# Two transformer blocks in fp32 on one Trainium2 core: layer ends taken token group by token group

## The chip, the cores and the metric

The kernel runs on one core of one Trainium2 chip. Its metric is the device time of one execution in microseconds (us), the median of several runs. Before the change it is 2314.95 us, over three runs from 2311.51 to 2321.45.

A core has these engines: TensorE (PE in the profile) for matrix products, VectorE (DVE), ScalarE (ACT) and GpSimd (POOL) for element-wise work, and SyncE (SP), which here only starts transfers. Each has its own instruction queue, and they wait for one another through semaphores. PE writes to PSUM, eight banks of 128 x 512 fp32 values. Everything else lives in SBUF.

## The reference, cut to what matters

The input x is 256 tokens by 2048 features in fp32. Two blocks follow each other. The first block is post-norm:

```python
x = layer_norm(ALPHA * x + attention_mixer(x, ...), ln_gain[0], ln_bias[0])
x = layer_norm(ALPHA * x + retention_mixer(x, ...), ln_gain[1], ln_bias[1])
```

The second block is pre-norm and is modulated by a vector c (mod is six rows of 2048 that come from c):

```python
h = rms_norm(x, norm_attn) * (1 + sc1) + sh1
x = x + g1 * (concat(window_attention(h), sparse_attention(h)) @ w_out)
h = rms_norm(x, norm_ffn) * (1 + sc2) + sh2
x = x + g2 * ((silu(conv(u)) * g) @ w_down)      # u, g = split(h @ w_up)
return rms_norm(x, norm_final)
```

So there are four places where a whole row of x must be finished, its mean square or variance taken, the row scaled, and only then may the next matrix product start (or the output be stored): after the attention mixer, after the retention mixer, after the second block's attention, and at the very end. They are called joins 1, 2, 3 and 4 here.

## The kernel before, in words

**Tiling.** The 256 tokens are NT = 2 groups of 128 (token 0 and token 1 below, index t). The residual x lives in `z[128, t, 2048]`. Weights come as blocks of 512 columns, each cut into CH = 4 chunks of [128, 4, 512] (1 MB). A chunk c of block b goes through these steps: SP loads it into `raw` (`load`, L353) once PE has finished chunk c of block b-1 (semaphore `products`), ACT rounds it to fp32r in `w_hi` (`round_hi`, L398), DVE writes the remainder to `w_lo` (`split_lo`, L403), and PE multiplies. A product of fp32 accuracy is three matmuls (`product`, L409 to L414: hi x hi, hi x lo, lo x hi).

**Projections.** `project` (L416) multiplies the activations x_hi and x_lo, kept transposed, with a block; chunk c covers four of the 16 row groups (kk) of the contraction and both token groups, so it is 24 matmuls. `output` (L440) is an output projection of one head group. Here chunk c is 512 output columns, and for each chunk PE does token 0 (12 matmuls), then token 1 (12 matmuls), into the PSUM banks `pair[c % 2][t]`. DVE then adds both banks to z (`vec_sum`, L1180; in the second block `vec_scaled_sum`, L2116, which multiplies by the gate row first and so takes four instructions per chunk).

**Order.** Nothing is planned at run time. The order of each engine is written out by hand, and every step waits on counts of semaphores. The three middle layers are hardware loops over heads or feed-forward groups. Around them stand single pieces for the first and the last head, and the joins lie in these pieces.

**A join before.** At joins 1 and 2 `vec_layer_end` (L1289) does for each of the four chunks the sum of both tokens and their `bn_stats`, with the split of the next block's chunk 0 after the first of them. After chunk 3 it aggregates both tokens at once, POOL takes one power -1/2 for both (`power`, L1475 and L2476), and at join 1 ACT normalizes token 0 in two halves (`act_normalize`, L940) and DVE token 1 (L1314). At join 2 DVE centres a whole token (L2139), scales it in two halves (L2145), and then does the other token; ACT takes the squares of each half as it comes (`act_rms`, L1849), and DVE and POOL make one rstd for both tokens. At joins 3 and 4 ACT squares each chunk once DVE has added it for both tokens (`act_squares`, L1855). From join 2 on `z_s`, the scaled copy of z, is made by ACT, with its first piece for token 1 made by DVE (L2105).

Then PE transposes the normalized row in eight groups j of 256 columns (`turn_groups`, L463): groups 0 to 3 at once and 4 to 7 between the matmuls of the first projection's chunk 0 (`turn_later`). For each group DVE applies gain and bias (x_mid, L517), ACT rounds (x_hi, L499), and DVE forms x_lo (L505), always two groups of x_mid and then their two x_lo (`turn_lo`, L501). The first projection's chunk c waits for 2(c+1) groups. `behind` in `turn_lo` puts the split of chunk 1 after group 3, and chunk 2 comes after group 7.

While the join runs, PE executes small matmuls on an identity matrix whose results nobody reads (`pe_fill`, L535): 22 at join 1, 71 at join 2, 28 at join 3.

**The end.** After the last chunk's sum DVE multiplies by the last norm's row (L2375), POOL takes the power, ACT scales token 0 and DVE token 1 in halves (L2086, L2449), and SP stores the four halves, token 0 and token 1 by turns (L2467).

## Time and profile before

| | |
|---|---|
| median of three runs | 2314.95 us (2311.51 to 2321.45) |
| the profiled execution: time, span | 2314.12 us, 2312.4 us |
| PE busy, share of the span | 2253.7 us, 97% |
| DVE busy | 1681.9 us, 73% |
| ACT busy | 993.3 us, 43% |
| POOL busy | 137.7 us, 6% |
| mean DMA rate | 218 GB/s |
| mean granted TensorE clock | 0.994 of full speed |

A single execution was profiled. Its time is 1.7 us longer than the span, which runs from the first to the last recorded event. PE's busy time contains the filling matmuls, so an engine that is 97% busy is not doing useful work for 97% of the span. "Idle before <- X" names what ended an engine's wait.

### The profile page before, as it was taken

How to read it: one execution, taken by the hardware profiler on the slowest of the kernel's cores; microseconds unless marked ns; L12 is line 12 of the kernel's file. 1: busy time of each engine (PE TensorE's matmuls, PEld its weight loads, DVE VectorE, ACT ScalarE, POOL GpSimd, SP SyncE). 2: the span in 40 equal slices, each digit the busy share in tenths (PEclk: the TensorE clock that was granted, in tenths of full speed). 3: DMA queues.
4: the chain of work that ended last, by engine and by line, in shares of the span. 5: the costliest groups of instructions: out<-in, count | busy, mean ns of one | idle time of the engine just before them, and what ended most of it. 6: DMA issues, size and time to landing. Idle time of an engine off the chain costs nothing.

```text
span 2312.4 us, 29071 instructions
## 1 busy us (share of the span) xinstructions
PE 2253.7 (97%) x10804; PEld 1861.2 (80%) x10804; DVE 1681.9 (73%) x1861; ACT 993.3 (43%) x1016; POOL 137.7 (6%) x197
## 2 busy tenths in 40 slices
PE   8999999999999999999999999999999999999997
PEld 6878888787888888888787778787888888888886
DVE  6788887978867878678785676984655666666567
ACT  4544443434434334343343456454444344444443
POOL 2101010010000000000001101000000000000000
PEclk9999999999999999999999999999999999999999
DMA  7777776587777777777745645454555555555553
GB/s 271 274 264 260 258 263 210 189 325 267 269 263 265 266 262 266 253 278 265 250 137 191 195 137 164 145 165 167 193 185 186 189 188 188 192 182 184 196 182 128
DMA packets 260289, 503.59 MB, mean 218 GB/s; under 512 B 14705, under 2 KB 68385, under 8 KB 259328
## 3 DMA queue, kind: packets, MB, share of 16 engines
q1 hardware_dynamic: 228480, 381.73, 48.9%
q0 software_dynamic: 31376, 119.80, 14.9%
q10 hardware_dynamic: 368, 1.18, 0.1%
q8 instruction: 42, 0.69, 0.1%
q14 instruction: 23, 0.19, 0.0%
HBM read 498.90 MB, written 3.69 MB: 217 GB/s over the span
## 4 chain that ended last, share of the span: by engine, by line
PE 53%; issue 36%; DVE 6%; DMA 3%; ACT 1%; POOL 0%; SPq 0%; DVEq 0%; ACTq 0%; POOLq 0%
PE pair_t L412 15%; PE pair_t L414 15%; PE pair_t L413 15%; DVE w_lo L406 1%; DMA raw<-in_attn_w_in_dram 1%; PE turn L532 1%; PE sc L776 1%; DVE m_acc L1026 1%; ACT w_hi L401 1%; PE sc L768 1%; DMA raw<-in_ret_w_in_dram 1%; PE sc L622 1%; PE sc L1572 1%; PE sc L640 0%; PE turn L1581 0%
## 5 line engine op out<-in xcount | busy, mean ns | idle before, releaser
L406 DVE TENSOR_TENSOR w_lo<-raw,w_hi 128x2048 fp32r<-128x2048 f32 (+1 forms) x367 | 822.5, 2243 | 495.2 <-ACT w_hi L401 491.0
L401 ACT ACTIVATE w_hi<-raw 128x2048 fp32r<-128x2048 f32 (+1 forms) x367 | 689.3, 1879 | 1068.7 <-DMA raw<-in_ret_w_in_dram 352.7
L412 PE MATMUL pair_t<-w_hi,x_hi 128*128 128x512 f32 (+1 forms) x2080 | 814.6, 392 | 17.1 <-DVE w_lo L406 9.7
L414 PE MATMUL pair_t<-w_hi,x_lo 128*128 128x512 f32 (+1 forms) x2080 | 799.3, 384 | 0.0
L413 PE MATMUL pair_t<-w_lo,x_hi 128*128 128x512 f32 (+1 forms) x2080 | 798.9, 384 | 0.0
L412 PEld LDWEIGHTS pair_t<-w_hi,x_hi 128*128 128x128 f32 x2080 | 393.0, 189 | 104.3 <-DVE w_lo L406 12.4
L414 PEld LDWEIGHTS pair_t<-w_hi,x_lo 128*128 128x128 f32 x2080 | 392.7, 189 | 78.2
L413 PEld LDWEIGHTS pair_t<-w_lo,x_hi 128*128 128x128 f32 x2080 | 393.2, 189 | 72.9 <-issue 0.2
L1026 DVE SCALAR_TENSOR_TENSOR m_acc<-m_raw,csilu,m_acc 128x1024 f32<-128x1024 f32 x180 | 230.7, 1282 | 7.0 <-DMA m_raw<-in_w_mod_dram 3.6
L412 PE MATMUL pair_t<-w_hi,f_hh 128*128 128x512 f32 x352 | 138.1, 392 | 0.3 <-DVE f_y L2120 0.3
L413 PE MATMUL pair_t<-w_lo,f_hh 128*128 128x512 f32 x352 | 137.1, 389 | 0.0
L414 PE MATMUL pair_t<-w_hi,f_hl 128*128 128x512 f32 x352 | 137.0, 389 | 0.0
L1467 POOL DMA_DIRECT2D m_raw<-in_w_mod_dram x96 | 69.0, 719 | 939.0 <-DVE m_acc L1026 924.1
L412 PE MATMUL pair_t<-w_hi,r_oh 128*128 128x512 f32 x256 | 102.8, 402 | 0.2
L414 PE MATMUL pair_t<-w_hi,r_ol 128*128 128x512 f32 x256 | 99.8, 390 | 0.0
L413 PE MATMUL pair_t<-w_lo,r_oh 128*128 128x512 f32 x256 | 99.6, 389 | 0.0
L412 PEld LDWEIGHTS pair_t<-w_hi,f_hh 128*128 128x128 f32 x352 | 66.1, 188 | 14.5 <-DVE f_y L2120 1.0
L414 PEld LDWEIGHTS pair_t<-w_hi,f_hl 128*128 128x128 f32 x352 | 66.1, 188 | 13.8
L413 PEld LDWEIGHTS pair_t<-w_lo,f_hh 128*128 128x128 f32 x352 | 66.1, 188 | 13.3
L1186 DVE TENSOR_TENSOR z<-z,pair_t 128x512 f32<-128x512 f32 x96 | 61.4, 681 | 16.0 <-PE pair_t L414 15.8
L2126 DVE TENSOR_TENSOR z<-z,f_y 128x512 f32<-128x512 f32 x88 | 56.9, 688 | 1.5
L412 PEld LDWEIGHTS pair_t<-w_hi,r_oh 128*128 128x128 f32 x256 | 48.1, 188 | 12.3 <-issue 1.7
(354 smaller groups left out, 2091.6 us busy)
## 6 DMA issues: line engine op xcount, KB each, us to landing
m_raw<-in_w_mod_dram POOLq DMA_DIRECT2D x96, 1024.0 KB, 6.3
raw<-in_ret_w_in_dram SPq DMA_DIRECT2D x192, 512.0 KB, 4.6
raw<-in_w_up_dram SPq DMA_DIRECT2D x176, 512.0 KB, 4.0
raw<-in_w_down_dram SPq DMA_DIRECT2D x88, 512.0 KB, 4.4
raw<-in_attn_w_in_dram SPq DMA_DIRECT2D x64, 512.0 KB, 4.5
raw<-in_ret_w_out_dram SPq DMA_DIRECT2D x64, 512.0 KB, 4.6
raw<-in_w_in_dram SPq DMA_DIRECT2D x56, 512.0 KB, 4.3
raw<-in_attn_w_out_dram SPq DMA_DIRECT2D x32, 512.0 KB, 5.6
```

The lines of the kernel that those rows point to most:

```text
L401: act.activation(chunk(w_hi, c, width), chunk(raw, c, width), ACT.Copy).then_inc(sem("hi"), 1)
L406: v.tensor_tensor(chunk(w_lo, c, width), chunk(raw, c, width), chunk(w_hi, c, width).bitcast(F32), ALU.subtract).then_inc(sem("lo"), 1)
L412: pe.matmul(to, xh, wh, start=start, stop=False)
L413: pe.matmul(to, xh, wl, start=False, stop=False)
L414: return pe.matmul(to, xl, wh, start=False, stop=stop)
L532: mm = pe.transpose(to[:, i * P:(i + 1) * P], src[:, t, m * P:(m + 1) * P], ident[:, :])
L622: mm = pe.matmul(sc[(h + 1) % 2][:, t * T:(t + 1) * T], a_qT[:, h, t * P:(t + 1) * P], a_kT[:, :], start=True, stop=True)
L768: mm = pe.matmul(sc[0][:, s * T:(s + 1) * T], r_kT[:, k, s * P:(s + 1) * P], r_qT[:, k, :], start=k == 0, stop=k == 1)
L1026: ins = v.scalar_tensor_tensor(out=m_acc[:, :], in0=w, scalar=cc, in1=m_acc[:, :], op0=ALU.mult, op1=ALU.add)
L1186: ins = v.tensor_tensor(z[:, t, c * CB:(c + 1) * CB], z[:, t, c * CB:(c + 1) * CB], pair[order[c]][t][:, :], ALU.add)
L1467: g.dma_start(m_raw[:, u % 2, :, :], w_m[:, 2 * u:2 * u + 2, bass.ds(2 * step * CB, 2 * CB)])\
L2126: ins = v.tensor_tensor(z[:, t, c * CB:(c + 1) * CB], z[:, t, c * CB:(c + 1) * CB], tmp[:, t, :], ALU.add)
```

## The change

The change touches the four joins only; the loops stay as they are.

- **Order on PE.** The last output projection of each layer calls `output_by_token`, which goes through `TOKENS`: chunks 0 and 1 as before, then chunk 2 token 0, chunk 3 token 0, chunk 2 token 1, chunk 3 token 1. Token 0's two late pieces are counted in `b_half`, token 1's in `products`.
- **Order on DVE.** Sums follow that order, and statistics, variance and rstd are taken for each token by itself. At joins 1 and 2 the split of the next block's chunk 0 moves behind the sums of chunk 1. At joins 3 and 4 `vec_tokens` takes the place of `vec_scaled_sum` in the last projection, and the split of the block's own chunk 3 moves ahead of all its sums.
- **POOL** takes one power per token (rsqrt counts to 10 rather than to 5).
- **ACT.** At join 1 it normalizes token 0, rounds chunk 1, then normalizes the first half of token 1 in two pieces. The squares of token 0 stand ahead of any scaling. At joins 3 and 4 token 0 is scaled in two halves while token 1 is still being summed.
- **Split of chunk 1 in two parts** (`split_half`): the first part ahead of the x_mid work (at join 2 both are), the second behind group 3. Chunk 2's split is behind group 5.
- **PE may start earlier:** the first projection's chunk 0 waits for one group of x_lo, and for the second only at its third row group (`pairs`).
- **Fills:** 22 to 12, 71 to 54, 28 to 15.
- **Stores** go token 0, then token 1, and ACT and DVE share token 1.

```diff
+        def split_half(v, b, c, h):
+            v.wait_ge(sem("hi"), CH * b + c + 1)
+            k = slice(2 * h, 2 * h + 2)
+            ins = v.tensor_tensor(w_lo[:, c, k, :], raw[:, c, k, :], w_hi[:, c, k, :].bitcast(F32), ALU.subtract)
+            if h == 1:
+                ins.then_inc(sem("lo"), 1)
@@ project
+                    if pairs and kk == 2:
+                        pairs()
@@
+        TOKENS = [(0, 0), (0, 1), (1, 0), (1, 1), (2, 0), (3, 0), (2, 1), (3, 1)]
+        def output_by_token(pe, b, oh, ol, before):
+            for c, t in TOKENS:
+                before(c, t)
+                if t == 0:
+                    pe.wait_ge(sem("lo"), CH * b + c + 1)
+                for k in range(CH):
+                    mm = product(pe, pair[c % 2][t][:, :], ..., c, k, CB, k == 0, k == CH - 1)
+                if t == 1:
+                    mm.then_inc(sem("products"), 1)
+                elif c > 1:
+                    mm.then_inc(sem("b_half"), 1)
@@ pe_a_output (pe_r_output, pe_f_output and the last output of the second attention alike)
+            def before_last(c, t):
+                if c < 2 and t == 0:
+                    before(c)
+                elif (c, t) == (2, 0):
+                    pe.wait_ge(sem("a_sum_z"), 2 + 4 * (i - 1) + 1)
+                elif (c, t) == (3, 0):
+                    pe.wait_ge(sem("a_sum_z"), 2 + 4 * (i - 1) + 2)
@@ pe_retention (the two other first projections alike)
-                    pe.wait_ge(sem("turn_lo"), 8 + 2 * (c + 1))
+                    pe.wait_ge(sem("turn_lo"), 8 + max(1, 2 * (c + 1) * (c > 0)))
+                    pairs=(lambda: pe.wait_ge(sem("turn_lo"), 10)) if first else None,
@@ pe_first_block, pe_second_block
-            pe_fill(pe, turn[0], 22)
+            pe_fill(pe, turn[0], 12)
-            pe_fill(pe, turn[0], 71)
+            pe_fill(pe, turn[0], 54)
-            pe_fill(pe, turn[0], 28)
+            pe_fill(pe, turn[0], 15)
@@ act_first_block
-            for c in range(3):
-                round_hi(act, R_B0, c)
-            act_normalize(act, 1, 1)
-            turn_hi(act, 1, False)
+            round_hi(act, R_B0, 0)
+            act_normalize(act, 0)
+            round_hi(act, R_B0, 1)
+            act_normalize(act, 1)
+            turn_hi(act, 1, False, range(0, 4))
+            round_hi(act, R_B0, 2)
+            turn_hi(act, 1, False, range(4, 8))
@@ vec_layer_end
+            for c in range(2):
+                vec_sum(v, which, base + c, CH * b + c + 1, c)
+                ...
+                for t in range(NT):
+                    vec(stat(t, c))
+            split_lo(v, b + 1, 0)
+            for c in range(2, CH):
+                token_sum(0, c)
+            variance(0)
             if which == "r":
+                centred(0)
+                for c in range(2, CH):
+                    token_sum(1, c)
+                variance(1)
+                scaled(0)
+                centred(1)
+                vec_rms(v, 1, 0)
+                scaled(1)
                 return
+            shift(0)
+            for c in range(2, CH):
+                token_sum(1, c)
+            variance(1)
+            shift(1)
+            zz = z[:, 1, 1024:2048]
+            v.tensor_scalar(zz, zz, mv[:, 1, 0:1], rstd[:, 1:2], ALU.subtract, ALU.mult)
@@ vec_first_block
+            split_half(v, R_B0, 1, 0)
+            turn_lo(v, 1, par[:, 0:KC], par[:, KC:2 * KC], behind={
+                3: lambda: split_half(v, R_B0, 1, 1), 5: lambda: split_lo(v, R_B0, 2)})
@@ second attention, join 2
+            act_rms(act, 1, 0)
+            round_hi(act, B_B0, 1)
+            act_rms(act, 1, 1)
+            act_scale_and_round(act, 1, B_B0)
...
+            split_half(v, B_B0, 1, 0)
+            vec_rms(v, 1, 1)
+            vec_scale(v, 1)
+            split_half(v, B_B0, 1, 1)
+            turn_lo(v, 2, aff[:, :], modc[:, 0:KC], behind={5: lambda: split_lo(v, B_B0, 2)})
@@ join 3
+            round_hi(act, B_B0 + 10, 3)
+            round_hi(act, f_block(0, 0), 0)
+            act_rms(act, 2, 0)
+            round_hi(act, f_block(0, 0), 1)
+            act_scale_first(act, 2)
...
+            act_rms(act, 2, 1)
...
+            split_lo(v, B_B0 + 10, 3)
+            vec_tokens(v, "b", 2, "b_scaled", 12, B_B0 + 10, b_tmp, 0, lambda: split_lo(v, f_block(0, 0), 0))
@@ join 4
+            act_rms(act, 3, 0)
+            act.wait_ge(sem("rsqrt"), 9)
+            act.wait_ge(sem("zw"), 6)
             for h in range(2):
                 act.activation(z[:, 0, w], f_zw[:, 0, w], ACT.Copy, scale=rstd[:, 0:1])
+            act_rms(act, 3, 1)
+            act.wait_ge(sem("rsqrt"), 10)
+            act.wait_ge(sem("zw"), 8)
+            act.activation(z[:, 1, 0:D // 2], f_zw[:, 1, 0:D // 2], ACT.Copy, scale=rstd[:, 1:2])
@@ vec_tokens (new; used at joins 3 and 4)
+            for c in range(2):
+                v.wait_ge(sem("products"), CH * b + c + 1)
+                vec(weighted(0, c))
+                counted(weighted(1, c), c)
+                vec(added(0, c))
+                full(added(1, c), c, 1)
+                if weigh: ...
+            if ahead:
+                ahead()
+            for c, t in TOKENS[4:]:
+                ... weighted, then added; token 0 after b_half, token 1 after products; weigh at join 4
+                if (c, t) == (3, 0):
+                    vec_rms(v, n, 0)
```

## Rows read from the trace of the kernel before

**Rows 1.** The page's part 1: busy time, share of the span, instructions.

```profile
PE 2253.7 (97%) x10804; PEld 1861.2 (80%) x10804; DVE 1681.9 (73%) x1861; ACT 993.3 (43%) x1016; POOL 137.7 (6%) x197
```

**Rows 2.** Waits of PE, whole span: total us, times, longest us.

```profile
PE pair_t L412 <- DVE x_lo L505: 5.7, 3, 2.1
```

**Rows 3.** Chain of waits, 398 to 416 us: start, us, what.

```profile
401.18 0.23 PE pair_t L413
...
401.67 1.30 DVE z L1186 x2
...
402.99 1.30 DVE stats L1298 x2
...
405.94 1.25 ACT z L944
...
407.23 0.67 PE turn L475 x4
...
407.93 1.91 DVE x_mid L517 x4
...
410.52 0.70 DVE x_lo L505
...
411.27 0.50 PE pair_t L412
```

**Rows 4.** Timeline of DVE around join 2: start, us, operation, [idle before <- releaser].

```profile
1170.66 2.29 DVE L406 TENSOR_TENSOR w_lo<-raw,w_hi 128x2048 fp32r<-128x2048 f32 x1 [1.09 <-ACT w_hi L401]
...
1183.13 2.35 DVE L2139 SCALAR_TENSOR_TENSOR z<-z,mv,rows 128x2048 f32<-128x2048 f32 x1
...
1190.93 2.48 DVE L2145 SCALAR_TENSOR_TENSOR z<-z,rstd,rows 128x1024 f32<-128x1024 f32 x2
```

**Rows 5.** Timeline of PE around join 2.

```profile
1200.79 0.50 PE L412 MATMUL pair_t<-w_hi,x_hi 128*128 128x512 f32 x1 [1.85 <-DVE x_lo L505]
...
1214.89 0.47 PE L412 MATMUL pair_t<-w_hi,x_hi 128*128 128x512 f32 x1 [1.11 <-DVE w_lo L406]
```

**Rows 6.** Timeline of POOL, at join 2 and in the attention layer.

```profile
1183.32 2.73 POOL L1482 TENSOR_TENSOR rstd<-var,minus_half 128x2 f32<-128x2 f32 x1 [22.80 <-DVE var L1306]
144.21 0.71 POOL L1482 TENSOR_TENSOR a_rs<-a_ss,minus_half 128x2 f32<-128x2 f32 x1 [1.53 <-DVE a_ss L1104]
```

**Rows 7.** Timelines of ACT, DVE and PE around join 3.

```profile
1526.56 1.92 ACT L401 ACTIVATE w_hi<-raw 128x2048 fp32r<-128x2048 f32 x1 [3.27 <-DMA raw<-in_w_out_dram]
1545.63 2.29 DVE L406 TENSOR_TENSOR w_lo<-raw,w_hi 128x2048 fp32r<-128x2048 f32 x1
1546.32 0.61 ACT L1859 ACTIVATE junk<-z 128x512 f32<-128x512 f32 x1
1549.11 1.95 ACT L1868 ACTIVATE z_s<-z,rstd 128x512 f32<-128x512 f32 x3 [2.09 <-POOL rstd L2478]
1553.99 0.50 PE L412 MATMUL pair_t<-w_hi,x_hi 128*128 128x512 f32 x1 [1.79 <-DVE x_lo L505]
```

**Rows 8.** Timelines of DVE, ACT and SP at the end.

```profile
2286.58 1.28 DVE L2120 TENSOR_TENSOR f_y<-pair_t,rows 128x512 f32<-128x512 f32 x2
2299.17 1.29 DVE L2120 TENSOR_TENSOR f_y<-pair_t,rows 128x512 f32<-128x512 f32 x2 [0.94 <-PE pair_t L414]
2304.47 2.19 ACT L2086 ACTIVATE z<-f_zw,rstd 128x1024 f32<-128x1024 f32 x2 [1.25 <-POOL rstd L2478]
2305.65 2.78 SPq L2467 DMA_DIRECT2D out_dram<-z  x4
```

**Rows 9.** Windows: PE, PEld, DVE, ACT, POOL busy (count), granted clock, DMA share, GB/s.

```profile
411.30:415.70 4.40, 4.40 (x12) 3.42 (x13) 4.30 (x7) 1.26 (x2) 0.00 (x0) 0.61 0.00 0
1549.20:1554.00 4.80, 2.16 (x17) 1.72 (x17) 3.66 (x8) 3.91 (x7) 0.00 (x0) 1.00 0.35 145
2307.00:2308.00 1.00, 0.00 (x0) 0.00 (x0) 0.00 (x0) 0.00 (x0) 0.00 (x0) 0.50 1.02 418
```

**Rows 10.** Timeline of PE's filling matmuls at join 3.

```profile
1542.78 6.41 PE L538 MATMUL turn<-ident 128*128 128x128 f32 x56
```

340 lines of the change are left out of this document (208 added, 132 removed).

## The prediction

> **What bounds the kernel now.** I read the page first: PE is busy 97% of the span [rows 1], so what a change can win lies in the stretches where PE waits or only fills. The table of PE's waits then shows how little there is of either: the longest entry that belongs to the joins is x_lo, 5.7 us in three waits [rows 2], one at each of joins 1 to 3. But a fill is not counted as a wait. So I followed the chain of waits through join 1 [rows 3]: last product, sum of two tokens (1.30 us), statistics of two tokens (1.30), power, ACT's normalization (1.25 for the half that is waited for), PE's transposes at 407.23, x_mid and x_lo, and PE's first real matmul at 411.27. PE's last product began at 401.41, one step of 0.23 us after the row at 401.18. Some 9.6 us of join 1 are therefore DVE, ACT and POOL in series, whatever PE does meanwhile. Join 2 is the same and longer: DVE centres (2.35) and scales (2.48) two tokens one after the other until 1193.41 [rows 4], and PE restarts at 1200.79, with one more stop of 1.11 us for chunk 2's split [rows 5]. Join 3 restarts at 1553.99 [rows 7]; join 4 ends in ACT's scaling and four stores [rows 8]. Elsewhere nothing is changed, and PE's share says that the layers between the joins are bound by PE, so what a join gives is kept.
>
> **Unit prices.** A matmul of 512 columns is 0.23 us apart from the next [rows 3], so one token of one output chunk (12 matmuls) is 2.72 us and a chunk 5.45. Sums, statistics, weighted and added pieces of one token are 0.65 each [rows 3, 8]. A whole split is 2.2 us of DVE's time (2.29 with its tail [rows 4, 7]), a half 1.15 (estimate: half of it). A power of two values is 0.71 beside products that read PSUM [rows 6]. Between statistics and normalization the chain of join 1 holds 0.94 us of small DVE instructions and hand-overs (402.99 + 1.30 = 404.29 to 405.94, less 0.71 for the power); with one token instead of two about 0.2 of the aggregation leaves, so I take 0.75, and 0.35 to 0.4 for two small instructions alone.
>
> **Join 1.** The order on PE puts token 0's last piece 2 x 2.72 us ahead of the end, so token 0's sums, statistics and normalization (DVE about 395.7 to 399.8, ACT to 402.2) lie beside token 1's products. After the last product remain one sum (0.65), one statistic (0.65), 0.75 + 0.71, and one quarter of token 1 on ACT (0.65): 401.65 + 3.4 = 405.05 instead of 407.23, a gain of 2.15. The moved rounding of chunk 1 lies on ACT at 402.2 to 404.1, inside that time. The first half split then stands between: it ends at 406.3, so x_mid starts 1.63 us earlier than 407.93, not 2.15. PE now waits for one x_lo and not for two: 0.70 less. PE restarts at 406.3 + 1.9 + 0.7 = 408.95 against 411.27: **2.3 us**. Bounds: 1.5, if the half split is a full one in cost, and 2.9, if it costs nothing. The splits of chunks 1 and 2 have more room than before. The wait of (3, 0) for chunk 1's sum is free, because chunk 0's split no longer stands ahead of that sum.
>
> **Join 2.** DVE is the series here. Chunk 1's sum and statistics end at about 1172.15, and the split that stood ahead of them, itself waiting 1.09 us for ACT [rows 4], follows to 1174.4. Then: two token 0 sums with statistics 2.6, variance 0.4, centring 2.35, the same two pieces for token 1 2.6 (the last product, at 1179.95, is there), 0.5, scaling 2.48, centring 2.35, 0.35, scaling 2.48. That is 1190.65 instead of 1193.41: 2.75 us. The squares follow each half as before. Splitting rstd by token lets ACT scale token 0's first piece before token 1's rstd, worth about 0.2. The two half splits cost: the first lies in DVE's wait for the squares, the second (1.15) delays x_mid by about 0.3 beyond what PE's transposes allow. One x_lo less is 0.70. PE restarts at 1197.6: 3.2 us. With chunk 2's split behind group 5 the 1.11 us stop [rows 5] goes too, for DVE reaches it at 1206.7 and PE needs it at 1210. **4.3 us**; bounds 3 and 5.5.
>
> **Join 3.** Here the gain was half taken already, since sums are added chunk by chunk and squares follow. DVE now splits chunk 3 first and has to wait for ACT until 1528.48 [rows 7], so the sums of chunks 0 and 1 end at 1536.05, next block's split at 1538.3, token 0's four pieces at 1541.0. ACT's square of it (0.61 + readout) ends at 1541.9. Then ACT rounds (1.92) and scales token 0 (2.2, as two halves of 1024 take [rows 8]) until 1546.0 and only then squares token 1, until 1547.35. Before, its last square started at 1546.32 [rows 7] and DVE's split held DVE until 1547.84. So rstd is 0.5 us earlier and no more: ACT is what is late next. DVE's first scaling of token 1 and the half split take 1.6 more, x_mid starts at 1550.25, PE restarts at 1552.9 against 1553.99: **1.1 us**; bounds 0 and 2.
>
> **Join 4.** New stall: (3, 0) needs the bank of chunk 1, whose weighted pieces DVE, late from its split, ends at 2286.58 + 3.9 + 1.3 = 2291.8 [rows 8]; PE could start at 2290.6. The last product is at 2300.25 instead of 2299.1. After it: DVE 2.1 to the added piece (it has 0.7 of earlier work left), square, 0.35, power 0.71: rstd of token 1 at 2304.7, half a token on ACT 1.15, first of its stores at 2305.9 against 2305.65. But two of the four stores are out long before. They are 2.1 MB at 418 GB/s [rows 9], 5.0 us in all, and 2.5 us of that leave the end: **2.1 us**; bounds 0.5 and 2.7.
>
> **The clock.** The fills are cut by more than the joins shorten. At join 3, 15 fills instead of 28 at 0.23 us each (6.41 us of them now [rows 10]) end at 1546.4, and PE then stands 2.8 us until its transposes, and again after them. In the trace the same pattern with a gap of 0.7 to 0.9 us ahead of the transposes and about 2 behind went both ways: at join 1 the granted clock fell to 0.61 in the mean of the next 4.40 us, in which 12 matmuls ran that take 2.76 at full clock [rows 9, 3], and at joins 2 and 3 it stayed at 1.00 [rows 9]. One fall costs 1.6 us. I count one more fall than before, at join 3, where the gap grows most; bounds: one fall fewer (+1.6) and two more (-3.3).
>
> **Sum.** 2.3 + 4.3 + 1.1 + 2.1 - 1.6 = 8.2 us. The profiled execution took 2314.12, so 2305.9 in its terms. The median is 0.8 above it: 2306.7, rounded to 2306.5. That is 0.36%, and about 0.5% (11.6 us, below 2303.4) is what a measurement of this kernel can tell from no change.
>
> **Rivals.**
> A, *the clock holds.* For it: two of the three joins kept it. Against: longer gaps at all three. Time: 2306.7 - 1.6, and another 1.6 if join 1's present fall goes: 2303.5. 24%.
>
> B, *POOL waits behind DVE.* At join 2 the power took 2.73 us instead of 0.71: it began 0.19 us after DVE's centring and ended 0.57 after it [rows 6, 4]. The powers for token 0 now fall into DVE's busiest stretch at joins 3 and 4. Each 2.0 late would hold ACT's scaling of token 0, and with it token 1's squares: 1.3 us at join 3 (there are 0.7 in hand), 1.9 at join 4, 3.2 together: 2310. Against: in both places a product from PSUM stands first, and beside such the power took 0.71 [rows 6]. The Trainium skill (SBUF — State Buffer, Who interferes with whom) says that a DVE instruction with two SBUF inputs and a GpSimd instruction that reads SBUF exclude each other for the whole instruction, the later one waiting, and that one SBUF input does no harm. By it the 2.73 us row is explained, the power slips in beside the weighted piece, and DVE's added piece waits some 0.1 us instead. 14%.
>
> C, *the gain is eaten later.* DVE has extra work in the first head after join 1 and in the second attention; if its splits set PE's pace there, joins 1 and 2 give half: 2310 to 2314. Against: no wait of PE for DVE is left there that is worth a microsecond. 7%.
>
> D, *slower.* The clock, once down, stays at 1.2 GHz through the first chunks, because the matmuls after the restart are themselves interrupted by transposes and waits. At half the clock a matmul costs about 0.2 us more (estimate: at most the 0.23 again); 9.8 us of gain are gone after 49 of them, two chunks in all. Two chunks slow at each of three joins less join 1's present fall would be 144 x 0.2 - 1.6 = 27 us at worst; one chunk at each, 72 x 0.2 - 1.6 = 12.8, which gives 2318. Against: the fall in the trace ended within 4.4 us. 5%.
>
> **Numbers.** Forecast 50%, A 24, B 14, C 7, D 5. Range 2300 to 2313.5: its low end is A with the joins' upper bounds in part, its high end most of B and C. Faster by over 0.5%: half of A and the low tail of the forecast, 25%; slower: D, 5%; within: 70%.
>
> **What would show it.** PE's first matmul comes 7.3 us after the last product at join 1 (before 9.6), 17.7 at join 2 (before 20.8), 9.9 at join 3 (before 11); no wait for the split of chunk 2 behind join 2; the granted clock below 1 behind join 3; powers of 0.71 at joins 3 and 4; a PE wait of 1.2 us for f_y ahead of chunk 3 in the last projection. Wrong would be: a wait of PE for DVE or ACT in the loops that was not there, a power over 2 us at joins 3 or 4, or stores that still end 6.7 us after the first of the last two is issued.

## The result and the profile after

The changed kernel takes **2298.9 us** (median of 7 runs, 2294.48 to 2302.05), against 2311.62 us for the kernel before (7 runs). The ratio is 0.993, with a 95% interval of 0.9916 to 0.9945. The forecast was 2306.5 us with a range from 2300.0 to 2313.5. The time lies below the range, and the change is faster by more than 0.5%, to which I had given 25%.

A later set of runs of the same kernel (e9) gave 2300.11 us, ratio 0.9943 (0.993 to 0.9957). The means of the two sets lie 15.9 and 14.3 us under those of before in the same sets; all 12 runs of after against the 48 runs of before that were taken beside the experiments give 14.9, give or take 2 (95%). I forecast 8.2.

Part 1 of the page of the changed kernel (its span is 2296.4 us), to be read against [rows 1]: PE works 11 us less, of which the 80 matmuls that are gone (two for each of the 40 fills, at 0.11 us each) make up about 9.

```profile
PE 2242.6 (98%) x10724; PEld 1851.6 (81%) x10724; DVE 1681.7 (73%) x1871; ACT 994.6 (43%) x1017; POOL 141.6 (6%) x202
```

PE's waits in the whole span of after (total us, times, longest), to be read against [rows 2]: the three waits for x_lo are 1.1 us shorter together, and there are two new entries for z_s, because the fills are fewer.

```profile
PE pair_t L420 <- DVE x_lo L515: 4.6, 3, 1.6
PE turn L485 <- DVE z_s L2256: 3.3, 2, 1.9
```

The timeline of PE in after. A row has start, duration, engine, line, operation, count, and in brackets the idle time ahead of it with the engine that ended it. First join 1, against the last rows of [rows 3], then join 2, against [rows 5], then join 3, against [rows 7, 10]:

```profile
403.94 2.84 PE L565 MATMUL turn<-ident 128*128 128x128 f32 x24
407.77 1.09 PE L485 MATMUL turn<-ident,z 128*128 128x128 f32 x8 [0.99 <-ACT z L996]
...
411.19 0.50 PE L420 MATMUL pair_t<-w_hi,x_hi 128*128 128x512 f32 x1 [1.45 <-DVE x_lo L515]
...
414.07 1.04 PE L485 MATMUL pair_t<-ident,z 128*128 128x128 f32 x8
...
1189.93 1.09 PE L485 MATMUL turn<-ident,z_s 128*128 128x128 f32 x8 [1.37 <-DVE z_s L2256]
...
1193.47 0.50 PE L420 MATMUL pair_t<-w_hi,x_hi 128*128 128x512 f32 x1 [1.58 <-DVE x_lo L515]
...
1532.68 3.51 PE L565 MATMUL turn<-ident 128*128 128x128 f32 x30
1538.10 1.09 PE L485 MATMUL turn<-ident,z_s 128*128 128x128 f32 x8 [1.92 <-DVE z_s L2256]
...
1541.65 0.50 PE L420 MATMUL pair_t<-w_hi,x_hi 128*128 128x512 f32 x1 [1.58 <-DVE x_lo L515]
```

A row's start alone says little here: at join 1 the changed kernel restarts at 411.19 against 411.27, but it had come to the join 2.5 us later, because of what happened in the first layer (below). So every join is measured from the end of its last product, which is where the fills begin. "Groups 4" is the start of the transposes of group 4, twelve matmuls behind the restart. In us:

| from the last product to | transposes | first matmul | groups 4 |
|---|---|---|---|
| join 1, before | 5.76 | 9.80 | 14.25 |
| join 1, after | 3.83 | 7.25 | 10.13 |
| join 2, before | 16.91 | 20.99 | 23.86 |
| join 2, after | 13.59 | 17.13 | 20.03 |
| join 3, before | 7.20 | 11.21 | 14.07 |
| join 3, after | 5.42 | 8.97 | 11.87 |

Windows of before (busy time and count of PE, PEld, DVE, ACT and POOL, granted clock, DMA share, GB/s), 4.4 us each: behind the restart of join 1, behind the transposes of i_q in the second attention, and behind those of f_g in the first feed-forward group. PE is busy throughout and gets through 12, 17 and 17 matmuls: the mean clock of each window is 0.61, part at 1.2 GHz and part at 2.4. Such a stretch at 1.2 GHz is called a fall of the clock here, and a stretch in which PE waits for another engine a stand.

```profile
411.30:415.70 4.40, 4.40 (x12) 3.42 (x13) 4.30 (x7) 1.26 (x2) 0.00 (x0) 0.61 0.00 0
1234.50:1238.90 4.40, 4.40 (x17) 3.78 (x18) 2.64 (x4) 2.12 (x2) 0.00 (x0) 0.61 0.54 189
1603.00:1607.40 4.40, 4.40 (x17) 3.77 (x18) 2.53 (x3) 4.15 (x3) 0.00 (x0) 0.61 0.45 171
```

The same three places in the profile of after, and join 3 as the third row: 23 or 24 matmuls, the clock at 1.00.

```profile
411.20:415.60 4.40, 4.40 (x23) 3.75 (x24) 4.26 (x8) 2.46 (x4) 0.00 (x0) 1.00 0.00 0
1225.80:1230.20 4.40, 4.39 (x24) 3.80 (x25) 2.67 (x4) 1.62 (x2) 0.00 (x0) 1.00 0.60 211
1541.70:1546.10 4.40, 4.40 (x23) 3.70 (x24) 4.30 (x8) 3.07 (x4) 0.00 (x0) 1.00 0.00 0
1590.90:1595.30 4.40, 4.40 (x24) 3.78 (x25) 2.54 (x3) 4.13 (x3) 0.00 (x0) 1.00 0.43 166
```

Each of these falls cost 1.6 to 1.7 us (the distance between two marks of PE around it, less the same in after). But they are not all the low clock that the two profiles have. Two more falls stand in both, near 50 and near 380 us, and after has two of its own in the first layer: its low clock at 49.8 us lasts twice as long as that of before, and one at 135.1 us has no counterpart. At the very end, where PE has nothing left to do, the clock falls too. Windows of before, then of after:

```profile
50.30:56.70 6.40, 6.40 (x31) 5.89 (x31) 6.36 (x5) 3.76 (x6) 0.76 (x1) 0.73 0.30 89
135.10:138.60 3.50, 3.50 (x17) 2.79 (x15) 3.46 (x3) 3.37 (x6) 0.74 (x1) 1.00 0.03 12
2303.10:2312.40 9.30, 0.00 (x0) 0.00 (x0) 1.77 (x5) 2.31 (x4) 0.69 (x1) 0.50 0.55 226
```

```profile
49.80:56.70 6.90, 5.12 (x24) 5.12 (x25) 5.99 (x6) 5.87 (x4) 0.00 (x0) 0.51 0.31 115
135.10:138.60 3.50, 3.45 (x8) 2.78 (x9) 3.34 (x6) 2.86 (x7) 0.00 (x0) 0.51 0.66 254
2292.40:2296.40 4.00, 0.00 (x0) 0.00 (x0) 0.00 (x0) 0.00 (x0) 0.00 (x0) 0.50 0.64 262
```

So before has five falls in its profile while PE works, and after four (counting its first low stretch as two): one fewer, and not three. The two of its own are the likely cause of the 2.5 us by which after came late to join 1. The 16.0 us between the two spans are therefore the three falls that are gone, 4.9 us, less those 2.5 us, and 13.6 us of other things; some 1.1 of these lie in parts that are not changed, the second layer's loops above all. **The order of the work is worth 12.5 us**: join 1 2.5 (4.12 less its fall), join 2 5.2 (from its last product to the transposes of m_acc behind chunk 3: 46.09 us before, 40.90 after), 0.3 ahead of join 2, join 3 2.2, join 4 2.3 (from one mark in the last feed-forward group to the end: 75.9 us before, 73.65 after).

### The profile page after: what moved, and what is told of

The parts are those of the page before. It is cut to its first block, busy times and chain, and to the rows that moved or that the text cites. A ratio compares the mean times of both kernels' runs of the same rounds, so it can differ in the third digit from the quotient of the medians.

```text
span 2296.4 us, 28927 instructions
## 1 busy us (share of the span) xinstructions
PE 2242.6 (98%) x10724; PEld 1851.6 (81%) x10724; DVE 1681.7 (73%) x1871; ACT 994.6 (43%) x1017; POOL 141.6 (6%) x202
## 4 chain that ended last, share of the span: by engine, by line
PE 85%; DVE 6%; DMA 4%; issue 2%; ACT 2%; SPq 0%; POOL 0%; DVEq 0%; POOLq 0%; ACTq 0%
PE pair_t L420 26%; PE pair_t L422 25%; PE pair_t L421 25%; DMA raw<-in_attn_w_in_dram 2%; PE turn L559 2%; DVE w_lo L406 1%; ACT w_hi L401 1%; PE sc L827 1%; PE sc L819 1%; DVE m_acc L1081 1%; PE sc L1678 1%; PE sc L677 1%; PE sc L659 0%; PE turn L1687 0%; DMA raw<-in_w_down_dram 0%
## 5 line engine op out<-in xcount | busy, mean ns | idle before, releaser
L1241 DVE TENSOR_TENSOR z<-z,pair_t 128x512 f32<-128x512 f32 x88 | 56.3, 681 | 14.5 <-PE pair_t L422 14.2
```

The source lines that it names most:

```text
L1241: ins = v.tensor_tensor(z[:, t, c * CB:(c + 1) * CB], z[:, t, c * CB:(c + 1) * CB], pair[order[c]][t][:, :], ALU.add)
```

## The experiments

Two theories about what was left over from 8.2 us. **Clock**: a fall comes out of a stand of PE, the change shortened the stands that count, and I had the sign of this term wrong. **Order**: the terms of joins 2 and 3 were too small. A rival to both: the falls are chance, and the profile of after was a lucky one. The mean clock is given for all runs of a kernel, since a profile is one run. 0.001 of it is 4.6 us of the span at half clock. Where PE is busy these cost it 2.3 us; where it has nothing to do they cost nothing. The idle end is such a place: it has 9.3 us at half clock in the profile of before and 8.8 in that of e1, but 4.1 and 6.9 in the two profiles of after, and 5.7 in the mean of all 15 profiles with the new end. The 3.4 us between the two means would count as 1.7 us of time won in a comparison of before and after, and are none.

| kernel | median us (runs) | ratio to before, 95% | mean clock |
|---|---|---|---|
| before | 2312.9, 2315.0, 2316.5, 2314.9 (48 runs in four sets) | 1 | 0.9939 |
| after | 2298.9 (7), 2300.1 (5) | 0.993, 0.9943 | 0.9950 |
| e1 before, short fills | 2317.55 (12) | 1.0012 (1.0003 to 1.0021) | 0.9910 |
| e2 no fills | 2297.98 (6) | 0.9924 (0.9911 to 0.9938) | 0.9917 |
| e3 gaps filled | 2300.51 (5) | 0.9936 (0.9923 to 0.995) | 0.9956 |
| e4 PE by chunk | 2304.55 (5) | 0.9956 (0.9943 to 0.9969) | 0.9940 |
| e5 long stands | 2304.62 (6) | 0.9956 (0.9942 to 0.997) | 0.9930 |
| e6 two x_lo | 2303.87 (6) | 0.9954 (0.9939 to 0.9969) | 0.9945 |
| e7 whole split | 2303.18 (5) | 0.9945 (0.9931 to 0.9958) | 0.9946 |
| e8 halves moved | 2297.99 (6) | 0.9926 (0.991 to 0.9941) | 0.9960 |
| e10 stands filled | 2294.83 (4) | 0.9906 (0.989 to 0.9921) | 0.9975 |
| e11 ACT's order | 2299.15 (5) | 0.9925 (0.9912 to 0.9939) | 0.9954 |
| e12 all | 2294.09 (4) | 0.9905 (0.989 to 0.992) | 0.9978 |
| e13 long stands, rest filled | 2298.6 (6) | 0.9932 (0.992 to 0.9944) | 0.9952 |

### e1: the kernel before with the new fill counts

```diff
-            pe_fill(pe, turn[0], 22)
+            pe_fill(pe, turn[0], 12)
...
-            pe_fill(pe, turn[0], 71)
+            pe_fill(pe, turn[0], 54)
...
-            pe_fill(pe, turn[0], 28)
+            pe_fill(pe, turn[0], 15)
```

> The kernel before with the new fill counts alone (12 instead of 22, 54 instead of 71, 15 instead of 28), nothing else of the change. Nothing that waits is moved, so PE's fills end 2.4, 4.0 and 3.1 us earlier and PE stands that much longer ahead of the transposes of joins 1, 2 and 3. Theory of the prediction (a longer stand ahead of the transposes brings clock falls): the granted clock after the restart is below 1 at join 3, where before it was 1.00, and probably at join 2; each fall costs 1.6 us, so 1.6 to 3.2 us slower than before, about 2314. Rival (falls come by chance and this gap has no say): the time of before, 2311.6 within the scatter, and the windows behind joins 2 and 3 at 1.00.

Measured: 3.1 us slower in the mean than before, mean clock 0.9910 instead of 0.9942. PE's timeline at join 2:

```profile
1197.99 1.94 PE L475 MATMUL turn<-ident,z_s 128*128 128x128 f32 x8 [4.69 <-ACT z_s L1868]
1199.72 1.91 PE L475 MATMUL sc<-ident,z_s 128*128 128x128 f32 x8
1202.53 0.80 PE L412 MATMUL pair_t<-w_hi,x_hi 128*128 128x512 f32 x1 [0.89 <-DVE x_lo L505]
...
1207.17 1.03 PE L475 MATMUL pair_t<-ident,z_s 128*128 128x128 f32 x8
```

and the windows of its transposes there and of its first matmuls:

```profile
1198.00:1202.00 4.00, 3.64 (x16) 3.24 (x16) 2.71 (x6) 2.58 (x5) 0.00 (x0) 0.50 0.01 2
1202.50:1206.50 4.00, 3.97 (x10) 3.16 (x11) 3.90 (x7) 2.97 (x5) 0.00 (x0) 0.52 0.00 0
```

After a stand of 4.69 us the transposes run at 1.2 GHz (1.94 us for eight, against 1.06), and so do the first products: from the last product to groups 4 it is 26.08 us instead of 23.86. At join 3 it is 16.46 instead of 14.07 after a stand of 3.70. The mechanism that I had forecast is real: a long stand does bring the clock down. The rival (the gap has no say) is out.

### e2, e3: no fills, and no gaps

e2 is after without the fills of joins 1 to 3. e3 has 17, 59 and 23 fills and six more behind the transposes of each join:

```diff
-            pe_fill(pe, turn[0], 12)
+            pe_fill(pe, turn[0], 17)
             turn_groups(pe, 1, lambda j: normalized(pe, j), False, range(4))
+            pe_fill(pe, pair[1][0], 6)
```

> The kernel after without the fills of joins 1, 2 and 3 (12, 54 and 15). PE then stands about 3.8, 13.6 and 5.4 us ahead of the transposes. If a stand brings the clock down, every one of the three joins has a granted clock below 1 behind its restart, and 1.6 us each make 4.8 us, about 2303.7; join 2 with its 13.6 us could cost more, because its transposes and copies run at the low clock too. Rival (stands have no say, falls are chance): 2298.9, with the clock at 1.00 behind most restarts.

> The kernel after with fills that reach to the transposes (17, 59 and 23 instead of 12, 54 and 15) and six more of 0.24 us each between the transposes and the first product of each of joins 1 to 3, where PE waits 1.45 to 1.58 us for x_lo. If the stands at the joins are what makes the clock fall, there is none at the joins, here and in every other run: up to 1.6 us per run less than after on the average, 2297.3 to 2298.9. Rival (the fills only lie in the way): each fill that runs past its time delays a restart by up to 0.3 us, 2299 to 2300, and falls show elsewhere as before.

Measured: e2 2297.98 us and e3 2300.51, neither told apart from after. e2 is the surprise. Its mean clock is 0.9917 against 0.9950, so it spent some 15 us more of its time at half clock than after, which could have cost 7.6 us, and it cost nothing that the times show. Its windows at join 2, with PE idle, in the transposes, in the first matmuls, and after them:

```profile
1180.00:1190.00 10.00, 0.00 (x0) 0.00 (x0) 9.34 (x14) 7.30 (x11) 4.05 (x4) 0.50 0.25 86
1190.70:1194.50 3.80, 3.69 (x17) 3.29 (x17) 3.59 (x6) 2.72 (x6) 0.00 (x0) 0.50 0.01 2
1194.50:1196.50 2.00, 2.00 (x5) 1.61 (x6) 1.97 (x5) 1.56 (x3) 0.00 (x0) 0.50 0.00 0
1196.50:1200.00 3.50, 3.50 (x21) 2.93 (x20) 2.79 (x7) 2.73 (x3) 0.00 (x0) 0.96 0.00 0
```

The clock falls while PE has nothing to do. The slow transposes lie where PE would wait for x_lo anyway. Only five products are slow, and from the last product to groups 4 join 2 takes 21.29 us instead of 20.03, join 1 10.41 instead of 10.13, join 3 12.61 instead of 11.87. My price of 1.6 us for every fall was wrong here: three falls cost 2.3 us in this profile. e3 has nearly the clock of after (0.9956), no fall at the joins of its profile, and its first matmuls come 7.25, 17.11 and 8.95 us after the last product, as in after: at the joins there was nothing left to save, and the fills did not delay a restart either. So the rival's "each fill delays a restart by up to 0.3 us" did not come true; 2300.51 lies within the scatter.

### e4: PE's order by chunk

```diff
-            for c, t in TOKENS:
+            for c, t in [(c, t) for c in range(CH) for t in range(NT)]:
                 before(c, t)
```

> The kernel after with PE's order of the four last projections by chunk again: (2,0) (2,1) (3,0) (3,1), everything else (DVE's order, squares, splits, scaling) as after. Token 0's last piece comes 2.72 us later. Theory (the order by tokens is what opens joins 1 and 4, less so 2 and 3, where DVE works in series): join 1 loses 2.0, join 2 1.1, join 3 0.9, join 4 2.2 us, together 6.2: about 2305. Rival (DVE's series decides, PE's order hardly): at most 2 us, 2301.

Measured: 2304.55 us. By the marks of PE join 1 loses 1.24 us (to groups 4), join 2 1.50, join 3 1.08, and from the last matmul to the end it is 10.81 us instead of 9.56: 1.25. Together 5.1, and the time agrees (the mean is 4.7 us above that of all 12 runs of after). The order by tokens is worth about 40% of what the joins gained; the rest lies in what DVE, ACT and POOL do. That it was 1.3 at joins 1 and 4 and not 2 to 2.2 I put down to DVE, which still had token 0's sum of chunk 2 to do either way; no run tests that. PE also stands longer ahead of the transposes here, 2.36, 2.67 and 2.90 us, and in the profile the clock fell in the transposes of joins 2 and 3, which is at most 0.25 and 0.1 us of the losses named.

### e5: stands as long as I had forecast

Fills 7, 48 and 11 instead of 12, 54 and 15.

> The kernel after with still fewer fills: 7, 48 and 11 at joins 1, 2 and 3 instead of 12, 54 and 15. PE then stands 2.2, 2.8 and 2.9 us ahead of the transposes instead of 0.99, 1.37 and 1.92. Theory (the prediction's clock term went wrong because the stand at join 3 came out as 1.92 us and not 2.8; a stand of 2.8 would have brought the clock down): at joins 2 and 3 the transposes or the first products run at half the clock, about 2 us each as in the first experiment: 2301 to 2303. Rival (a stand of 2.8 us is still harmless, falls begin only near the 3.7 us that the first experiment had at join 3): clock 1.00 there and 2298.9.

Measured: 2304.62 us, ratio 0.9956, mean clock 0.9930: 4.6 us slower in the mean than after. But the profiled run was one of its fastest, with a single fall at the joins, inside the transposes of join 3, which delays the restart by 0.16 us, two others at i_q and f_g, and two in the first layer. So it was open where the slow runs had lost their time (see e13).

### e6: two x_lo again

```diff
-                    pe.wait_ge(sem("turn_lo"), 8 + max(1, 2 * (c + 1) * (c > 0)))
+                    pe.wait_ge(sem("turn_lo"), 8 + 2 * (c + 1))
```

The same at joins 2 and 3, and `pairs` is gone.

> The kernel after, but PE's first product waits for two x_lo at each of joins 1 to 3, as before, not for one. Theory (the prediction's term of 0.70 us for one x_lo holds): each restart is 0.7 us later, together 2.1 us: 2301.0. Rival (PE would stop for the second x_lo in the middle of chunk 0 otherwise, so it is only moved): the join's end, where PE transposes groups 4 and 5, stays where it is, and 2298.9.

Measured: 2303.87 us, more than the 2301.0 of the theory. From the last product to the first matmul it is 8.04, 17.90 and 9.76 us: 0.79, 0.77 and 0.79 later. At joins 1 and 3 groups 4 come 0.76 and 0.75 later, so the gain is not given back, and my 0.70 was nearly right. Beside it the stand ahead of the first matmul is 2.24 to 2.37 us, longer even than the 1.79 to 2.07 of before, and at join 2 the clock fell behind it (groups 4 at 22.24 us instead of 20.03).

### e7, e8: the half splits

e7 has chunk 1's split whole and in one place. e8 keeps the halves and moves the ones that stand ahead of x_mid:

```diff
-            split_half(v, R_B0, 1, 0)
             turn_lo(v, 1, par[:, 0:KC], par[:, KC:2 * KC], behind={
-                3: lambda: split_half(v, R_B0, 1, 1), 5: lambda: split_lo(v, R_B0, 2)})
+                1: lambda: split_half(v, R_B0, 1, 0), 3: lambda: split_half(v, R_B0, 1, 1),
+                5: lambda: split_lo(v, R_B0, 2)})
```

> The kernel after with chunk 1's split whole and in one place again: at join 1 and join 3 ahead of the transposed columns, at join 2 in DVE's wait for the squares. Theory (at joins 1 and 3 the split stands on the path, at join 2 beside it): x_mid starts 1.15 us later at joins 1 and 3; at join 2 the first split ends at 1189.4 instead of 1188.3, ahead of rstd, but the second half that stood ahead of x_mid is gone, so up to 0.1 us is won there: +2.2 us, 2301. Rival (DVE catches up behind the joins and PE's later stops shrink by as much): 2299.

> The kernel after with the half splits that stand just ahead of x_mid put elsewhere: join 1's first half behind the transposed columns of group 1, join 2's second half behind group 3, join 3's first half ahead of the root of token 1, where DVE stands 1.26 us for the squares. Theory (in the kernel after, x_mid follows the half split and not PE's transposes: the split ends at 1191.01 and PE's first transposes of join 2 at 1190.5): restarts 0.35, 0.5 and 0.5 us earlier, 2297.5. Rival (PE's first transposes set x_mid anyway, the half split is hidden as the prediction nearly had it, 0.3 us at join 2): 2298.9, and at join 1 a new stop at chunk 1 because its split comes later.

Measured, e7: the first matmul comes 1.07, 0.73 and 1.04 us later, so a half split costs what I had estimated (1.15) where it lies on the path. At join 2 I had the whole split as free; the transposes came 0.95 us later. The clock was low behind the restarts of all three joins of its profile, but it did not fall in the same place at each: at join 1 it fell in the stand ahead of the first product (2.52 us), at joins 2 and 3 already in the transposes, after stands of 2.32 and 1.90 us. Join 3:

```profile
1538.49 1.19 PE L485 MATMUL turn<-ident,z_s 128*128 128x128 f32 x8 [1.90 <-DVE z_s L2256]
1539.47 1.91 PE L485 MATMUL sc<-ident,z_s 128*128 128x128 f32 x8
```

Measured, e8: the restarts are 0.17, 0.22 and 0.32 us earlier, and the time is that of after within the interval. Of the 1.15 us of a half split that is little: the rest is hidden behind PE's transposes, more than the prediction had at join 1 (where it let 0.5 us show) and about as it had it at join 2 (0.3). The theory written for e8 was too large. Join 2 gives its part back in a new stop of 0.49 us for m_acc.

### e9, e10: after again, and the stands elsewhere filled

```diff
             pe_a_turn(pe, A_KV)
+            pe_fill(pe, sc[0], 5)
             pe_a_output(pe, A_KV)
...
                 if c == 0:
+                    pe_fill(pe, turn[0], 7)
                     pe.wait_ge(sem("i_q"), 1)
...
+                    if first:
+                        pe_fill(pe, sc[0], 9)
                     pe.wait_ge(sem("f_g"), f + 1)
```

> The kernel after once more, unchanged, beside the next three, to have its own scatter and clock on the same chip. Nine profiles so far show clock falls in places that the change does not touch, after stands of 2.0 to 2.7 us ahead of the transposes of i_q and of f_g, some runs with and some without at the same length of stand. Theory (whether a fall comes there is chance, and the profiled run of after had three fewer than that of before by luck in part): this profile shows at least one fall there, the mean clock over the runs is 0.995 as before, and the time about 2299. Rival (the kernel after is free of them because of where its instructions lie): the profile is free of them again.

> The kernel after with fills in three stands that the change does not touch: 7 of 0.24 us each ahead of the wait for i_q (stand 2.04 us), 9 ahead of the first wait for f_g (2.66 us), and 5 between the transposes and the products of the last output projection of the first attention (1.57 us). Theory (each fall comes out of a stand and costs 1.6 us): no fall in these three places, mean clock 0.997 to 0.998 instead of 0.995, and 2 to 3 us less than the kernel after on the same chip. Rival (falls come by chance wherever PE stands a little, or the stands do not make them): mean clock 0.995 and the time of after.

Measured: e9 2300.11 us, e10 2294.83, on the same chip. Windows of e9 behind i_q and f_g, against the second and fourth window of after above:

```profile
1224.30:1228.70 4.40, 4.40 (x18) 3.61 (x19) 2.66 (x4) 1.87 (x2) 0.00 (x0) 0.65 0.58 203
1590.70:1595.10 4.40, 4.36 (x16) 3.84 (x17) 2.62 (x3) 4.17 (x3) 0.00 (x0) 0.61 0.46 176
```

It is the same program, with the same stand of 2.04 us ahead of i_q to the hundredth, and the clock fell in one run and not in the other. So two of the three falls of before that the profile of after lacks were luck; the two that it has in the first layer were the opposite. The stand still matters. Over all profiles, a stand of 2.03 us or more ahead of i_q ended in a fall in 8 of 9, and stands of 2.43 to 2.71 us ahead of f_g in 8 of 12; the three stands of 0.86 to 1.79 us at i_q, and the ten places at i_q and f_g with fills, had none. In e10 fills bring it to 0.59 us at i_q and 0.66 at f_g:

```profile
1222.56 1.72 PE L565 MATMUL turn<-ident 128*128 128x128 f32 x14
1224.87 1.09 PE L559 MATMUL turn<-ident,i_q 128*128 128x128 f32 x8 [0.59 <-ACT i_q L2048]
```

```profile
378.00:382.00 4.00, 3.29 (x23) 2.91 (x24) 1.62 (x4) 2.89 (x3) 2.06 (x3) 1.00 0.53 178
1224.80:1229.20 4.40, 4.33 (x23) 3.74 (x24) 2.74 (x4) 2.02 (x3) 0.00 (x0) 1.00 0.57 199
1589.80:1594.20 4.40, 4.37 (x23) 3.76 (x24) 2.62 (x3) 4.26 (x3) 0.00 (x0) 1.00 0.43 168
```

The mean clock rises to 0.9975 and the mean time is 7.4 us under that of e9 (5.3 between the medians), more than I had expected. "Chance" was half the truth: whether a fall comes is chance, that it can come is the stand. How short a stand must be is not shown: ahead of the first attention's last output projection, after stands of 0.84 and 1.57 us with 1.1 us of transposes between them, the clock fell in 5 of 12 profiles (none of 5 with fills), and e10's own profile has three falls left in the first layer.

### e11, e12: ACT's order at join 3, and everything together

```diff
             act_rms(act, 2, 0)
-            round_hi(act, f_block(0, 0), 1)
-            act_scale_first(act, 2)
+            act_scale_first(act, 2, 0)
...
             act_rms(act, 2, 1)
+            act_scale_first(act, 2, 1)
```

The last argument is the half that is scaled, and chunk 1 is now rounded in `act_rms`, ahead of the squares of token 0's chunk 2.

> The kernel after with another order of ACT at join 3: next block's chunk 1 is rounded ahead of the squares of token 0's chunks 2 and 3, while ACT stands, and the second half of token 0's scaling follows token 1's squares instead of preceding them. Nothing else. Theory of the prediction (at join 3 ACT is what is late: it comes to token 1's squares only after rounding and scaling): the last square starts when DVE's last piece is there, 1535.3 instead of 1535.82, and the restart is 0.5 us earlier, 2298.4. Rival (DVE's series sets join 3): nothing, or the second half of the scaling, now behind, delays x_hi: 2298.9 to 2299.5.

> Half splits moved as in the eighth run (0.17, 0.22 and 0.32 us at the restarts of joins 1 to 3 there), ACT's order at join 3 as in the run before this, and the three stands filled. Theory: 0.7 + 0.5 + 2 to 3 us less than the kernel after on the same chip, about 2295.5. Rival (only the structure adds up, the clock's part is chance): 1.2 us less, 2297.7.

DVE's row ahead of the root of token 1 in after says what it waits for:

```profile
1536.56 0.16 DVE L2246 TENSOR_REDUCE mv<-ssq 128x1 f32<-128x4 f32 x1 [1.70 <-ACT junk L1987]
```

In e11 the same row:

```profile
1537.80 0.16 DVE L2248 TENSOR_REDUCE mv<-ssq 128x1 f32<-128x4 f32 x1 [0.58 <-ACT junk L1989]
```

The wait is 1.12 us shorter, and from the last product to the first matmul join 3 takes 7.84 us instead of 8.97. ACT was what was late, as the prediction said, by twice what I had expected of this run. Two things were moved at once, the rounding and the second half of the scaling, and this run does not tell their shares apart. In the times it is not told apart from e9 (2299.15 against 2300.11). e12 takes 2294.09 us, 1% under the kernel before and the fastest of all. Its last step over e10 lies within the scatter. Its profile has join 3 at 7.99 us and not less, because the half split that e8 puts ahead of the root no longer fits into a wait of 0.58: the root follows it without a wait, 3.20 us after the last product, where it came after 2.76 in e11.

### e13 to e15: long stands with all others filled

> The stands at joins 1 to 3 as long as in the fifth run (fills 7, 48 and 11: 2.2, 2.8 and 2.9 us ahead of the transposes), and the three other stands filled as in the tenth, so that low clock can only come from the joins. To be read against the tenth run (2294.8 us, mean clock 0.9975). Theory (stands of 2.2 to 2.9 us at the joins bring falls that reach into the products, and are what made the fifth run 3 to 4 us slower than after): mean clock 0.994 to 0.995 and 3 to 5 us more, about 2298.5, with a fall in the profile at one of the three restarts. Rival (the fifth run lost its time in the places that are filled here; at the joins the low clock lies in the transposes, which PE has time for, 0.2 us each): mean clock 0.996 to 0.997 and at most 1 us more, 2295.5.

> The same kernel, a second profile, to see at which of the three joins the clock is low and whether the low part reaches past the restart. Theory: at least one restart in the three profiles whose first products take 0.79 instead of 0.50 us and whose twelve products ahead of group 4's transposes take over 4 us instead of 2.87. Rival: falls only in the transposes, restart at most 0.3 us late.

> The same kernel, a third profile; expected as for the second.

Measured: 2298.6 us against 2294.83 of e10 (on another chip), means 4.1 us apart, mean clock 0.9952 against 0.9975. The first profile has falls at all three joins. PE at joins 1 and 3:

```profile
404.01 1.19 PE L485 MATMUL turn<-ident,z 128*128 128x128 f32 x8 [2.11 <-ACT z L997]
404.99 1.91 PE L485 MATMUL sc<-ident,z 128*128 128x128 f32 x8
407.43 0.80 PE L420 MATMUL pair_t<-w_hi,x_hi 128*128 128x512 f32 x1 [0.52 <-DVE x_lo L515]
...
412.26 1.03 PE L485 MATMUL pair_t<-ident,z 128*128 128x128 f32 x8
...
1538.82 1.97 PE L485 MATMUL turn<-ident,z_s 128*128 128x128 f32 x8 [2.81 <-DVE z_s L2260]
1540.58 1.91 PE L485 MATMUL sc<-ident,z_s 128*128 128x128 f32 x8
```

Groups 4 come 1.95, 1.99 and 1.23 us later than in after. In the two further profiles the clock stays up at joins 2 and 3, with the same stands of 2.65 to 2.79 us, and falls at join 1 for 0.25 and 0.10 us. The times and the mean clock are as the theory had them; the profiles are divided, one as the theory and two as the rival had it. Had the stand at join 3 been the 2.8 us that I forecast, a fall would have been possible, not certain: with stands of 2.79 to 2.90 us there (e4, e5, e13, e14, e15) the clock fell in three of five profiles, and it delayed groups 4 by 0.1 us (e5) to 1.2 us (e13), not by the 1.6 that I had counted.

## Why the prediction was wrong

The forecast was 8.2 us, and over the runs it is about 15. By its own steps:

- **The clock, the step that failed.** "I count one more fall than before, at join 3": -1.6. That fall did not come, and the one that before has at join 1 is gone: in the six profiles that have the early x_lo, the half splits, PE's order by token and the fill counts of after (after, e8 to e12) the clock stays at 1.00 at all 18 joins. At the joins, profile against profile, the term is +1.6 instead of -1.6. Over the runs the mean clock rose from 0.9939 to 0.9950 (the rise is 0.0003 to 0.0019 at 95%), 2.5 us, of which some 1.7 are the shorter idle end, where low clock costs nothing. That leaves about 0.8 us, give or take 2: the term is off by about 2.4 us, and its sign over all runs is open.

  Two things were wrong in it. The stand at join 3 was put at 2.8 us and is 1.92 [against rows 10], since the transposes came 5.4 us after the last product and not 6.4. And I priced the stand ahead of the transposes, which grew, and took the one ahead of the first product as unchanged ("and again after them"), while it fell from 2.07, 1.85 and 1.79 us to 1.45, 1.58 and 1.58, because PE waits for one x_lo. I had priced the x_lo at 0.70 us and not seen that it also shortens a stand.

  In the nine joins with a wait for two x_lo, or for a whole split ahead of it (before, e6, e7), the clock fell five times: three times behind that second stand, when it was 2.07, 2.37 and 2.52 us long (and not at two others of 2.24 and 2.37), and twice in e7 already in the transposes. That this second stand is the cause is read from these counts and not shown; no run changed it alone without moving the restart, and e7's join 3 fell after a first stand of 1.90 us, as long as that of after.
- **Join 3, mis-sized**: 1.1 forecast, 2.2 measured. The mechanism was right (e11). ACT's squares of token 1 ended 3.9 us after the last product, where I had 4.6: ACT ended the square of token 0 and began its rounding 0.5 us earlier than I had worked out. From there to x_mid it was 2.5 us, where I had 2.9.
- **Join 2, mis-sized**: 4.3 forecast, 5.2 measured, and 0.3 ahead of it. DVE's series came out to 0.1 us: its last scaling ends 10.8 us after the last product, forecast 10.7 (the terms as written add up to 0.15 less). What was more: 0.5 from there to the transposes where I had 0.2, 0.54 to the first matmul (0.4), and 1.33 behind it, where the stop of 1.11 us [rows 5] went with a little besides.
- **Join 1 and join 4 right**: 2.5 against 2.3 forecast, and 2.3 against 2.1. At join 4 that is in part luck: PE's last product comes 1.8 us later than before, counted from the mark in the last feed-forward group, where I had 1.15 (0.5 us of it is a longer stop one projection earlier, which varies from run to run), and the end follows it after 9.2 us where I had 10.1. The new stop ahead of chunk 3 is there, 0.84 us instead of 1.2:

```profile
2278.73 0.50 PE L420 MATMUL pair_t<-w_hi,f_hh 128*128 128x512 f32 x1 [0.84 <-DVE f_y L2261]
```

  and two of the four stores are out early, as said. SP's row, then ACT's scaling of the two tokens, against [rows 8]:

```profile
2287.68 5.33 SPq L2646 DMA_DIRECT2D out_dram<-z  x4
```

```profile
2286.50 2.19 ACT L2233 ACTIVATE z<-f_zw,rstd 128x1024 f32<-128x1024 f32 x2 [1.03 <-POOL rstd L2657]
...
2291.02 1.15 ACT L2238 ACTIVATE z<-f_zw,rstd 128x1024 f32<-128x1024 f32 x1 [1.03 <-POOL rstd L2657]
```

- **Rival A** (the clock holds, 24%) is what happened at the joins, and the time went below its own: its 2303.5 stands on joins that were priced 2.7 us too low. It was right about the joins; over all runs its clock gain of 1.6 to 3.2 us is more than the mean clock leaves (about 0.8).
- **Rival B** (POOL waits behind DVE) did not come true at joins 3 and 4: the power of one value took 0.56 us at join 3 and 0.54 at join 4. At join 2, where DVE centres and scales, POOL's rows show it:

```profile
1174.50 2.60 POOL L1586 TENSOR_TENSOR rstd<-var,minus_half 128x1 f32<-128x1 f32 x1 [17.13 <-DVE var L1373]
1179.88 1.54 POOL L1586 TENSOR_TENSOR rstd<-var,minus_half 128x1 f32<-128x1 f32 x1 [2.78 <-DVE var L1373]
...
1188.79 0.56 POOL L2657 TENSOR_TENSOR rstd<-var,minus_half 128x1 f32<-128x1 f32 x1 [1.90 <-DVE var L2250]
```

  The first two begin beside a DVE instruction of 2.34 and of 1.24 us and end after it, the last has DVE to itself. (A fourth, between them at 1184.80, took 1.53 us beside a scaling of DVE.) They cost nothing there, since DVE and ACT come to what needs them later still. By the Trainium skill (SBUF — State Buffer, Who interferes with whom) the two exclude each other when DVE reads two SBUF inputs and GpSimd reads SBUF, and the trace agrees at joins 2, 3 and 4: beside DVE's product from PSUM, with one input in SBUF, the power took 0.56 and 0.54 us.
- **Rivals C and D**: no wait of PE for DVE appeared in the loops that was not there before. In the profiles of after and e9 no clock is low at the joins, so D had nothing to stand on. What it feared is not impossible: in e1, behind joins 2 and 3, the first products ran at half clock after a stand of 3.7 to 4.7 us.

Of the 6.8 us that the forecast was short, about 2.4 are the clock (give or take 2), 2.7 are the joins (2.3 of them joins 2 and 3), and about 1.7 were not traced; in the two profiles 1.1 us lie in parts that the change does not touch. The range was too narrow at its low end: the low end took the joins' upper bounds only in part, and with the joins as measured (12.5) and no fall added or lost the time would have been 2302.4 by the forecast's own way of counting, 2300.8 with one fall fewer.

## What to carry to other kernels

A wait that an edit shortens is worth its own length and the risk of a clock fall that hung on it; add up each engine's idle stretches ahead of PE's restarts before and after, all of them, not only the one that the edit names. Fills pay where they bring a stand of 2 to 3 us under 1 us (e10: 5 to 7 us for 21 fills), and did nothing that the times show where most of the low clock lay in idle time and in transposes that PE had time for (e2). When one profile is set against one other, list the falls of both over the whole span, not only at the places compared, and take them out of the difference first: here three were gone, 4.9 us, and two others had come. And take the idle end out of the mean clock before it is read as time.

## What the runs showed of the hardware that was not expected

- The same stand, the same program, either outcome: 2.04 us ahead of i_q in after and in e9, clock at 1.00 in one and at 0.65 in the other.
- Low clock that lies in idle time is free: e2 spent some 15 us more at half clock than after (mean clock 0.9917 against 0.9950), at the same time.
- After 13.44 us of idling the low clock lasted for the first 6 us after PE's restart (1190.71 to about 1196.8 in e2); after the short stands of before it was gone within 4.4 us.
- Beside no DVE instruction with two inputs in SBUF, the power of one value takes 0.54 to 0.57 us on POOL, of two values 0.69 to 0.72; beside such instructions 1.53 to 2.73.
